# The experts' down product in three fp32r terms throughout, with POOL making part of its operands

## What is computed

```python
def one_group(args):          # xg: 128 rows of one expert
    xg, e = args
    return (jax.nn.silu(xg @ w_gate[e]) * (xg @ w_up[e])) @ w_down[e]   # 1024 -> 256 -> 1024
```

## Time and profile before

| | |
|---|---|
| median of 3 runs | 1967.78 us (1967.21 to 1970.19) |
| the profiled execution | 1968.77 us, span 1967.1 us |
| mean granted clock of TensorE | 0.972 |
| busy: PE, PEld, DVE, ACT, POOL | 1878.7, 1432.8, 1139.2, 793.0, 250.9 us |
| the fp32 matmul of the down product (L2442) | 103.6 us in 200 instructions |

### The profile page before, as it was taken

The page is one execution under the profiler, slowest core; times in us unless marked ns, Lnnn a source line. Parts: engine busy times, 40 slices in busy tenths (PEclk is TensorE's granted clock), DMA queues, the critical chain, the costliest instruction groups (busy, mean ns, idle before and its releaser), DMA issues.

```text
span 1967.1 us, 30340 instructions
## 1 busy us (share of the span) xinstructions
PE 1878.7 (96%) x9317; PEld 1432.8 (73%) x9318; DVE 1139.2 (58%) x1995; ACT 793.0 (40%) x1427; POOL 250.9 (13%) x336
## 2 busy tenths in 40 slices
PE   5999999999899999999899999995999999999987
PEld 2788778877567777777688888884677777777732
DVE  3777777777530000003555555556688888888748
ACT  3445445544320010003111211122577777777722
POOL 0111011101000000000111101111122222222211
PEclk7999999999899999999999999997999999999989
DMA  9212222222574445546534444435888645789987
GB/s 379 97 77 109 108 77 88 109 108 82 190 249 171 181 175 194 194 174 248 211 136 147 149 142 146 149 107 182 301 305 301 223 141 185 270 300 361 326 299 324
DMA packets 175594, 379.56 MB, mean 193 GB/s; under 512 B 32236, under 2 KB 104092, under 8 KB 168352
## 3 DMA queue, kind: packets, MB, share of 16 engines
q1 hardware_dynamic: 137520, 318.05, 44.8%
q0 software_dynamic: 20560, 52.32, 7.0%
q10 hardware_dynamic: 17472, 8.66, 1.5%
HBM read 293.58 MB, written 103.73 MB: 202 GB/s over the span
## 4 chain that ended last, share of the span: by engine, by line
PE 64%; DVE 4%; DMA 2%; issue 1%; ACT 1%; ACTq 1%; SPq 0%; DVEq 0%; POOL 0%; POOLq 0%
PE fin L160 17%; PE fin L162 17%; PE fin L161 17%; PE fin L2442 4%; PE fin L2409 2%; PE fin L1764 2%; PE fin L1803 1%; PE fin L1256 1%; PE fin L2454 1%; DVE expert_gate_up L2385 1%; DVE expert_gate_up L2389 1%; ACTq L2025 1%; DMA w_out_raw<-in_w_o 1%; DVE expert_down L2378 1%; DMA w_gate_raw<-in_w_in 1%
## 5 line engine op out<-in xcount | busy, mean ns | idle before, releaser
L2313 DVE TENSOR_TENSOR gate_up_lo<-expert_gate_up,gate_up_hi 128x2048 fp32r<-128x2048 f32 x98 | 223.7, 2287 | 12.5 <-ACT gate_up_hi L2198 12.0
L2198 ACT CAST gate_up_hi<-expert_gate_up 128x2048 fp32r x98 | 188.3, 1923 | 87.9 <-issue 84.6
L160 PE MATMUL mix<-w_mix_hi,hT_hi 128*128 128x512 f32 (+3 forms) x544 | 203.7, 375 | 3.8 <-DVE hT_lo L601 2.5
L1166 DVE SCALAR_TENSOR_TENSOR ma_rows<-tanh_rows,fin 128x512 f32<-128x512 f32 x32 | 20.6, 683 | 310.2 <-PE fin L162 159.8
L161 PE MATMUL mix<-w_mix_hi,hT_lo 128*128 128x512 f32 (+3 forms) x544 | 199.3, 366 | 0.0
L162 PE MATMUL mix<-w_mix_lo,hT_hi 128*128 128x512 f32 (+3 forms) x544 | 198.8, 365 | 0.0
L160 PE MATMUL fin<-gate_up_hi,gathered_T_hi 128*128 128x512 f32 x400 | 160.4, 401 | 3.0 <-DVE gathered_T_lo L2304 1.6
L162 PE MATMUL fin<-gate_up_lo,gathered_T_hi 128*128 128x512 f32 x400 | 156.3, 391 | 0.0
L161 PE MATMUL fin<-gate_up_hi,gathered_T_lo 128*128 128x512 f32 x400 | 155.6, 389 | 0.0
L160 PEld LDWEIGHTS mix<-w_mix_hi,hT_hi 128*128 128x128 f32 (+1 forms) x544 | 100.9, 185 | 37.1 <-issue 20.3
L162 PEld LDWEIGHTS mix<-w_mix_lo,hT_hi 128*128 128x128 f32 (+1 forms) x544 | 100.9, 186 | 19.2
(11 more groups left out here) (359 smaller groups left out, 3980.5 us busy)
## 6 DMA issues: line engine op xcount, KB each, us to landing
expert_gate_up<-in_w_gate SPq DMA_DIRECT2D x32, 1024.0 KB, 7.5
expert_gate_up<-in_w_up SPq DMA_DIRECT2D x32, 1024.0 KB, 11.6
expert_down<-in_w_down SPq DMA_DIRECT2D x32, 1024.0 KB, 12.4
h_parts<-hT_split SPq DMA_DIRECT2D x16, 1024.0 KB, 5.1
mixer_parts<-oT_split SPq DMA_DIRECT2D x32, 512.0 KB, 8.2
w_ada_part<-in_w_ada SPq DMA_DIRECT2D x16, 1024.0 KB, 10.6
h_parts_b<-hT_split SPq DMA_DIRECT2D x16, 1024.0 KB, 4.9
expert_down<-weighted_rows SPq DMA_DIRECT2D x12, 1024.0 KB, 8.4
```

The lines of the kernel that those rows point to most:

```text
L160: nc_mm(out, left[0], right[0], start=first, stop=False)
L1166: last = nc.vector.scalar_tensor_tensor(out=ma[:, par, at], in0=tg[:, at], scalar=1.0, in1=ps[2 + n][:, :], op0=ALU.add, op1=ALU.mult)
L2198: nc.scalar.copy(wg[par][0][:, n * HG:(n + 1) * HG], ring[:, bass.ds(slot * GU + n * HG, HG)]).then_inc(w_hi, 1)
L2313: nc.vector.tensor_tensor(wg[par][1][:, at], ring[:, bass.ds(slot * GU + n * HG, HG)], wg[par][0][:, at].bitcast(F32), ALU.subtract).then_ ...
```

## The change

The down product's second half is done like its first, in three fp32r terms. For that the high part of the down weights now covers both halves (two casts on ACT, the second half's first), DVE makes the low part of the first half as before, and POOL makes that of the second half in a new step `rest_low(b)`, behind the scatter of block b-1. PE waits for one more semaphore. The hidden activations are copied in one piece of 256 columns, and their low part has that width too. The turned expert rows have one pair of buffers (high and low) in place of two, so ACT's write of the pair waits for the gate/up product of the block before. One register load goes from ACT's step and one from PE's; POOL's step gains one.

```diff
@@ experts: buffers and semaphores
-    xT = [[sb(f"gathered_T{n}_{part}", [P, KD, P], F32R) for part in ("hi", "lo")] for n in range(2)]
+    xT = [sb(f"gathered_T_{part}", [P, KD, P], F32R) for part in ("hi", "lo")]
-    hT = [sb(f"hidden_T_{part}", [P, P], F32R) for part in ("hi", "lo")]
-    hT_rest = sb("hidden_T_rest", [P, P])
-    wd = [sb(f"down_{part}", [P, D], F32R) for part in ("hi", "lo")]
+    hT = [sb(f"hidden_T_{part}", [P, 2 * P], F32R) for part in ("hi", "lo")]
+    wd = [sb(f"down_{part}", [P, DOWN], F32R) for part in ("hi", "lo")]
+    rest_hi, rest_lo = sem("e_down_rest_hi"), sem("e_down_rest_lo")
@@ on_gpsimd
+        def rest_low(b):
+            slot = listed(pool, 0, b)
+            pool.wait_ge(rest_hi, b + 1)
+            pool.tensor_tensor(wd[1][:, D:], downs[:, bass.ds(slot * DOWN + D, D)], wd[0][:, D:].bitcast(F32), ALU.subtract).then_inc(rest_lo, 1)
+
         def step(b, slot, landed):
             gather(b + 2, (slot + 2) % 4, landed)
             scatter(b - 1, (slot - 1) % 4)
+            rest_low(b)
...
         gather(2, 2, 16)
+        rest_low(0)
...
             scatter(fore * 2 + 2 + n - 1, slot)
+            if n < 2:
+                rest_low(fore * 2 + 2 + n)
@@ on_scalar
         def turned(b, slot, more=True):
-            par = slot % 2
             act.wait_ge(x_turned, b + 1)
-            if not isinstance(b, int) or b > 1:
-                act.wait_ge(gu, b - 1)
+            if not isinstance(b, int) or b > 0:
+                act.wait_ge(gu, b)
             for n in range(2):
-                last = nc.scalar.copy(xT[par][0][:, 4 * n:4 * n + 4, :], ps[n][:, :].rearrange("p (k m) -> p k m", m=P))
+                last = nc.scalar.copy(xT[0][:, 4 * n:4 * n + 4, :], ps[n][:, :].rearrange("p (k m) -> p k m", m=P))
...
-        def weights(b, par, parts=(0, 1)):
-            slot = listed(act, 0, b)
+        def weights(b, par, parts=(0, 1), slot=None):
+            slot = listed(act, 0, b) if slot is None else slot
...
         def hidden(b, par):
...
-            nc.scalar.activation(hT[0][:, :], ps[4][:, 0:P], ACT.Copy, scale=0.5)
-            nc.scalar.activation(hT_rest[:, :], ps[4][:, P:2 * P], ACT.Copy, scale=0.5).then_inc(hT_ready, 1)
+            nc.scalar.activation(hT[0][:, :], ps[4][:, 0:2 * P], ACT.Copy, scale=0.5).then_inc(hT_ready, 1)
         def down_high(b):
...
-            nc.scalar.copy(wd[0][:, :], downs[:, bass.ds(slot * DOWN, D)]).then_inc(d_hi, 1)
+            nc.scalar.copy(wd[0][:, D:], downs[:, bass.ds(slot * DOWN + D, D)]).then_inc(rest_hi, 1)
+            nc.scalar.copy(wd[0][:, 0:D], downs[:, bass.ds(slot * DOWN, D)]).then_inc(d_hi, 1)
...
-            weights(b + 2, par, (0,))
+            place = weights(b + 2, par, (0,))
             weigh(b - 1, (slot - 1) % 4, landed, before)
             hidden(b, par)
             down_high(b)
-            weights(b + 2, par, (1,))
+            weights(b + 2, par, (1,), place)
@@ on_vector
-            nc.vector.tensor_tensor(wd[1][:, :], downs[:, bass.ds(slot * DOWN, D)], wd[0][:, :].bitcast(F32), ALU.subtract).then_inc(d_lo, 1)
+            nc.vector.tensor_tensor(wd[1][:, 0:D], downs[:, bass.ds(slot * DOWN, D)], wd[0][:, 0:D].bitcast(F32), ALU.subtract).then_inc(d_lo, 1)
...
-            nc.vector.scalar_tensor_tensor(out=hT[1][:, :], in0=ps[4][:, 0:P], scalar=0.5, in1=hT[0][:, :].bitcast(F32),
+            nc.vector.scalar_tensor_tensor(out=hT[1][:, :], in0=ps[4][:, 0:2 * P], scalar=0.5, in1=hT[0][:, :].bitcast(F32),
@@ on_tensor
-        def out(b, par):
-            slot = listed(pe, 0, b)
+        def out(b):
             pe.wait_ge(d_lo, b + 1)
+            pe.wait_ge(rest_lo, b + 1)
             pe.wait_ge(hT_lo, b + 1)
...
             for n in range(2):
-                at = slice(n * 512, (n + 1) * 512)
-                three(nc.tensor, ps[5 + n][:, :], (hT[0][:, :], hT[1][:, :]), (wd[0][:, at], wd[1][:, at]), True, False)
-                last = nc.tensor.matmul(ps[5 + n][:, :], hT_rest[:, :], downs[:, bass.ds(slot * DOWN + D + n * 512, 512)], start=False, stop=True)
+                for k in range(2):
+                    at, rows = slice(k * D + n * 512, k * D + (n + 1) * 512), slice(k * P, (k + 1) * P)
+                    last = three(nc.tensor, ps[5 + n][:, :], (hT[0][:, rows], hT[1][:, rows]), (wd[0][:, at], wd[1][:, at]), k == 0, k == 1)
             last.then_inc(down, 1)
```

More of the change, by code:

```diff
@@ L2198, in weights @@
                 nc.scalar.copy(wg[par][0][:, n * HG:(n + 1) * HG], ring[:, bass.ds(slot * GU + n * HG, HG)]).then_inc(w_hi, 1)
+            return slot
         def silu(b, par):
@@ L2300, in on_vector, with turned @@
     def on_vector(dve):
-        def turned(b, par):
+        def turned(b):
             dve.wait_ge(xT_hi, b + 1)
             for n in range(2):
-                last = nc.vector.tensor_tensor(xT[par][1][:, 4 * n:4 * n + 4, :], ps[n][:, :].rearrange("p (k m) -> p k m", m=P),
-                                               xT[par][0][:, 4 * n:4 * n + 4, :].bitcast(F32), ALU.subtract)
+                last = nc.vector.tensor_tensor(xT[1][:, 4 * n:4 * n + 4, :], ps[n][:, :].rearrange("p (k m) -> p k m", m=P),
+                                               xT[0][:, 4 * n:4 * n + 4, :].bitcast(F32), ALU.subtract)
             last.then_inc(xT_lo, 1)
@@ L2334, in step @@
             silu(b, par)
-            turned(b + 1, 1 - par)
+            turned(b + 1)
             weights(b + 1, 1 - par, (1,))
@@ L2344, in on_vector @@
             nc.vector.tensor_tensor(wg[0][1][:, at], ring[:, at], wg[0][0][:, at].bitcast(F32), ALU.subtract).then_inc(w_lo, 1)
-        turned(0, 0)
+        turned(0)
         weights(1, 1)
         silu(0, 0)
-        turned(1, 1)
+        turned(1)
         weights(2, 0, (0,))
@@ L2364, in on_vector @@
         silu(b, 0)
-        turned(b + 1, 1)
+        turned(b + 1)
         weights(b + 1, 1, (1,))
@@ L2420, in gate_up @@
                 at = slice(k * 2 * EH, (k + 1) * 2 * EH)
-                last = three(nc.tensor, ps[2 + par][:, :], (xT[par][0][:, k, :], xT[par][1][:, k, :]),
+                last = three(nc.tensor, ps[2 + par][:, :], (xT[0][:, k, :], xT[1][:, k, :]),
                              (wg[par][0][:, at], wg[par][1][:, at]), k == 0, k == KD - 1)
@@ L2447, in step @@
             turn(b + 1, 1 - par, n)
-            out(b - 1, 1 - par)
+            out(b - 1)
             turn_h(b, par)
@@ L2476, in on_tensor @@
         gate_up(fore * 2 + 3, 1)
-        out(fore * 2 + 2, 0)
+        out(fore * 2 + 2)
         turn_h(fore * 2 + 3, 1)
-        out(fore * 2 + 3, 1)
+        out(fore * 2 + 3)
         total = listed(pe, TOTAL, 0)
```

## The result

The changed kernel takes **2026.62 us** (median of 4 runs, 2024.80 to 2028.08), the kernel before 1968.3; the ratio is 1.0289, 95% interval 1.0277 to 1.0302. Forecast were 2011 us and a range up to 2024. The direction was right; the loss is 58 us where 43 were expected, and the time lies above the range. The profiled execution took 2028.08 us, its span is 2025.1. Shown first is the experts' window, then the line of tanh (L2211 now); they answer to the earlier trace rows.

What follows compares the result with a forecast made beforehand. TensorE was taken to bound the kernel, others following closely. At 10.58 a block against 9.73, 48 blocks add 40.8 us and the last block 2.4: 1968.8 becomes 2012.0, less 1.0 for the median, 2011 us; range 1976 to 2024.

Steps and rivals of the forecast that it cites:

- TensorE, 0.32 us less a block: Down product: six fp32r products replace four and the fp32 ones; PE alone would go at 9.41 us a block.
- ACT, 9.47 a block: ACT's block queue: the extra cast adds 0.95 us; two blocks take at least 18.93, or 9.47 a block.
- the issue gap: ACT's wait for its own sequencer before gate/up's high part: 0.22 longer on average, once in two blocks; 10.47 becomes 10.58.
- One pair for the turned rows at zero: ACT's new wait on gate/up sits behind a tanh waiting for the same count: cost zero.
- At +8.94 POOL finds the down low part running (+8.70 to +9.93) and starts at +9.95: Times after the block's tanh: POOL's subtraction follows DVE's down low part, ending +12.09; two blocks take 20.94.
- POOL's length: POOL's 128x1024 subtraction: 2.14 us, from two selects (1.28) and a stream at the memset's slope (0.86).
- the signs named for being wrong: POOL row near 1 us; DVE and POOL unslowed together; down waits released by DVE or ACT; DVE gate/up low parts over 2.3.
- The last block: Stage's open end: about 3.1 us later, product about 0.7 shorter, so 2.4 more.
- no collision: First rival: POOL's subtraction reads beside DVE's work; 10.08 a block, 16.8 us more, 1987 us; chance 0.14.
- The faster one: Second rival: POOL's result is in time, its operation under 1.45 without collision; ACT decides, 9.58 a block, 1961 us; chance 0.11.
- Gathers were not late: Third rival: POOL issues the gather at +12.39; one in four late by one us, 12 more, 2023 us; chance 0.10.
- The losses did not cancel PE's gain: Fourth rival, whole change: losses cancel PE's gain, so it doesn't bite, 1968 us; chance 0.03.

Runs made afterwards that it cites:

- e10: Changed kernel without the second down-weight cast and POOL's subtraction, second half's terms reusing the first half's weights: 1952.77 us, ratio 0.9919 to the kernel before.
- e1: Changed kernel without POOL's subtraction, leaving out the low part of the second half's weights: 1964.8 us, ratio 0.9981 to the kernel before.
- e5: Kernel before with one pair of buffers for the turned rows and nothing else: 1969.78 us, ratio 1.0000.
- e8: Changed kernel with POOL's subtraction ahead of the scatter of the block before: 2008.87 us, ratio 1.0193 to the kernel before.
- e3: Changed kernel with ACT's two down-weight casts in the other order, first half then second: 1996.9 us, ratio 1.0141 to the kernel before.
- e4: Kernel before with one pair for the turned rows and an idle POOL subtraction per block that nobody waits for: 1970.57 us, ratio 1.0007.
- e2: Changed kernel with a memset of the same tile in place of POOL's subtraction: 1965.46 us, ratio 0.9981 to the kernel before.
- e9: Changed kernel with POOL's subtraction made to wait until DVE's down low part of the same block is finished: 2028.28 us, ratio 1.0297 to the kernel before.

## Why the prediction was right and where it failed

- TensorE, 0.32 us less a block: right. e10 gives 9.38 against 9.41.
- ACT, 9.47 a block and 9.58 with the issue gap: right in size, 9.63 in e1. The casts end at +8.72 against +8.64.
- One pair for the turned rows at zero: right (e5). One copy for both hidden halves is in e10 as well and leaves PE's term whole; its step on ACT is 0.35 (1584.98 to 1585.33), not 0.26.
- POOL's subtraction and DVE's down low part in line are what decides: right, though it is DVE's result that comes last. Taking the subtraction away gives 62 us (e1). That the two exclude each other is shown by e8 and e3, where each engine in turn is the one held, by e4, where POOL is held and nobody waits, and by e2, where a write holds nobody. The Trainium skill (SBUF — State Buffer, Who interferes with whom) says that a GpSimd instruction which reads and a DVE instruction with two SBUF inputs exclude each other and that one which only writes is exempt; e8, e3 and e2 agree, with 2.59, 2.62 and 1.23 us.
- What failed is the step "At +8.94 POOL finds the down low part running (+8.70 to +9.93) and starts at +9.95", with the claim that "either order puts 1.23 and 2.14 in line". POOL goes first: +9.28 to +11.69, and DVE's remaining 1.09 comes behind it, so the pair ends at +12.78 instead of +12.09. By itself that order would have cost next to nothing: from a scatter that ends at +8.64, 2.41 and 1.09 give about +12.15, an estimate from these rows. But it brings a later start with it, which I had put at nothing. Because DVE's down_lo is held, DVE's whole queue moves back: the turned rows' low part starts at +2.70 instead of +1.98, the gate/up low part ends at 1587.01, +8.38, and the scatter that waits for it (below) ends at +9.27 instead of +8.64. These 0.63 are nearly all of the 0.69 that are too much. In e9, where DVE isn't held, the scatter ends at +8.65. I had costed the wait on DVE, and not what is queued behind it.
- POOL's length was short too: 2.40, not 2.14. Half of the figure of the Trainium skill (GPSIMD Engine Reference, Performance versus the Vector engine), an estimate of 2.25, was the better value, and the memset and select rows a poor stand-in (the two memsets lead to 0.97 for 1024 columns, not 0.95, and e2 measured 0.98). In the order of the sum it would have mattered little, since 2.24 of it come after DVE's end (e3), where the sum had 2.16.
- In time: +12.78 instead of +12.09 is 0.35 a block, some 17 us over 48, of which the issue gap that I had allowed for gives a part back (10.84 a block measured, 10.58 forecast: 12.5 us). One of the signs named for being wrong is there: the waits before the down product are released by DVE, not by POOL.
- The last block: forecast 2.4 us, measured 3.6. From the last tanh to the start of y it takes 17.09 (1923.95 to 1941.04), before 13.51 (1871.27 to 1884.78). The rows of PE and of ACT answer to the earlier trace rows:

```profile
1935.54 0.76 PE L160 MATMUL fin<-down_hi,hidden_T_hi 128*128 128x512 f32 x1 [7.13 <-DVE hidden_T_lo L2339]
```

```profile
1923.95 0.38 ACT L2211 ACTIVATE tanh_e<-fin 128x256 f32<-128x256 f32 x1 [2.00 <-PE fin L162]
1928.37 1.27 ACT L2233 ACTIVATE y_block<-fin,row_records 128x512 f32<-128x512 f32 x2 [4.03 <-PE fin L162]
...
1941.04 1.27 ACT L2233 ACTIVATE y_block<-fin,row_records 128x512 f32<-128x512 f32 x2 [8.66 <-PE fin L162]
```

The down product starts 11.59 after the tanh instead of 7.36: 4.23 later, where 3.1 was forecast. Of these 1.18 are there already when ACT scales the result of the block before (4.42 after the tanh, before 3.24), and the other 3.05 are the forecast's. Then it takes 5.50 at half clock (0.50 from 1935 to 1941, the 1.2 GHz level) instead of 6.15, the 0.7 less that was expected.
- The rivals: no collision would have been 1987 and fell. The faster one needed POOL's operation under 1.45. Gathers were not late in the changed kernel; they were in e8. The losses did not cancel PE's gain either.
- PE's waits of 1.2 us a block did not cost the clock: 0.99.

Left open: why POOL's subtraction goes first although DVE's row starts 0.42 before POOL's. The traces bound it: in the changed kernel POOL goes first with DVE's row up to 0.50 ahead; in e4, where the subtraction follows the scatter just as closely, DVE goes first with its row 0.75 to 0.80 ahead, and in e3 with 0.67 or more. It may be that POOL takes the port before its row starts, in the tail of the scatter; no run here separates that from a row that is drawn late.

## What to carry to other kernels

Before work goes to the idle GpSimd, lay both engines on one clock: a GpSimd subtraction that reads SBUF and a VectorE operation with two SBUF inputs run one after the other. What it ran beside here with neither longer was VectorE work that takes one of its two inputs from PSUM (e4). The price falls on whoever comes second. When a row is held, move its engine's whole queue back before reading off when everything else starts. And cost an exchange of engine times by the chain of the block, not by busy shares: POOL was 23% busy before, and giving it 2.4 us a block cost 1.1.

## What was not expected of the hardware

An indirect DMA's instruction on POOL waits for DVE as well. Where it starts during a DVE operation of two SBUF inputs, its row ends 0.87 to 0.92 after that operation, in 46 of the changed kernel's scatters and 47 of its 48 gathers. In the block above the scatter ends at 1587.90 and DVE's gate/up low part at 1587.01, the gather at 1592.31 and DVE's down_lo at 1591.41. They are 1.91 and 1.83 us long there, and the same gather takes 1.03 in e9, where no such DVE operation runs. The kernel before has it too, unnoticed: its scatter lasts 1.27 and its gather 1.06, and both end late in the same way.

And POOL's subtraction of 128x1024 takes 2.36 to 2.40 us where the memset of that size takes 0.98. The idle one of e4, with fp32 out and one tile as both inputs, takes 1.91 where nothing holds it. How much of the difference is the reading and how much the arithmetic, no run separates.
